# Reordered combinations, modulation rows first, score head pairs, and the state table loaded ahead of the lag table

## The reference, cut to what matters

```
# first block, 512 tokens x 1024 channels
proj = rms_norm(h) @ w_in                        # q, k, v, g, u
scores = einsum(q, k) * decay                    # 8 heads of 64
ret = silu(g) * group_norm(scores @ v)
h = h + concat([ret, pool_mixer(u)]) @ w_out
h = h + moe(rms_norm(h))                         # top 4 of 32 experts
gate = sigmoid(rms_norm(h, norm_ple_w) @ ple_gate_w)
h = h + gate * (p @ ple_proj_w)
x = rms_norm(h, final_norm_w)
# second block, layer 0: 64 groups of a complex state space model
u = modulate(rms_norm(x), shift, scale)
state_t = Abar * state_{t-1} + Bbar * u_t        # 64 states per group
y = gelu(Re(C state_t) + D * u_t)
x = x + g1 * (y @ w_out)[value * sigmoid(gate)]
# then feed-forward, short convolution, feed-forward, final norm
```

## Time and profile before

| | us |
|---|---|
| median of 3 runs | 2770.83 (2763.73 to 2775.92) |
| the profiled execution, its own time | 2767.87 |
| its span, first to last instruction | 2766.2 |
| PE busy in the span | 2596.2 |
| DVE busy | 1962.1 |
| ACT busy | 1352.4 |
| mean granted TensorE clock | 0.968 of full |

### The profile page before, as it was taken

How to read it: one execution, slowest core, us unless ns; L and a number is a source line. 1 busy time by engine, 2 the same in 40 slices (tenths; PEclk the granted TensorE clock), 3 DMA queues, 4 the chain that set the end, 5 groups by cost and what they waited for, 6 DMA issues and landing times.

```text
span 2766.2 us, 34756 instructions
## 1 busy us (share of the span) xinstructions
PE 2596.2 (94%) x12400; PEld 2103.0 (76%) x12400; DVE 1962.1 (71%) x1968; ACT 1352.4 (49%) x1346; POOL 187.7 (7%) x288
## 2 busy tenths in 40 slices
PE   5988889999999999999998786989999999999998
PEld 4767768888888888888886356878888787788886
DVE  5767789999999999999999877467743444533432
ACT  4232467777777777777776253322232222322322
POOL 1214010000000000000000200011100000000000
PEclk9999889999999999999999898999999999999999
DMA  6762599999999999999996932357743532133332
GB/s 231 259 209 48 208 343 389 381 382 381 384 379 380 380 383 383 384 381 380 382 379 231 181 86 71 81 152 227 222 108 87 145 91 76 31 100 97 97 105 73
DMA packets 364565, 642.30 MB, mean 232 GB/s; under 512 B 40908, under 2 KB 234132, under 8 KB 363732
## 3 DMA queue, kind: packets, MB, share of 16 engines
q1 hardware_dynamic: 341172, 541.28, 57.9%
q0 software_dynamic: 17296, 76.03, 8.0%
q10 hardware_dynamic: 6032, 24.12, 2.2%
HBM read 615.22 MB, written 26.68 MB: 232 GB/s over the span
## 4 chain that ended last, share of the span: by engine, by line
PE 85%; DVE 8%; DMA 3%; ACT 2%; issue 1%; POOL 0%; DVEq 0%; ACTq 0%; SPq 0%; POOLq 0%
PE bank L2384 38%; PE bank L2612 12%; PE bank L2613 12%; PE bank L2618 12%; PE bank L2484 1%; DMA cb<-in_w_ada 1%; PE bank L2359 1%; PE bank L2372 1%; PE bank L2366 1%; PE bank L2193 1%; PE bank L2244 1%; PE bank L2194 1%; PE bank L2195 1%; PE bank L2236 1%; DVE rows L1812 1%
## 5 line engine op out<-in xcount | busy, mean ns | idle before, releaser
L1709 DVE TENSOR_TENSOR slot_lo<-ring,slot_hi 128x2048 fp32r<-128x2048 f32 x384 | 864.0, 2284 | 84.0 <-ACT slot_hi L1001 82.8
L1001 ACT ACTIVATE slot_hi<-ring 128x2048 fp32r<-128x2048 f32 x384 | 736.3, 1920 | 283.9 <-PE bank L2384 259.2
L2384 PE MATMUL bank<-slot_hi,xs_hi 128*128 128x512 f32 x1024 | 324.5, 398 | 0.0
L2384 PE MATMUL bank<-slot_hi,xs_lo 128*128 128x512 f32 x1024 | 317.0, 391 | 0.0
L2612 PE MATMUL bank<-h_hi,fin_hi 128*128 128x512 f32 x704 | 277.3, 394 | 4.1 <-ACT h_hi L1214 3.4
L2613 PE MATMUL bank<-h_hi,fin_lo 128*128 128x512 f32 x704 | 275.6, 391 | 0.0
L2384 PE MATMUL bank<-slot_lo,xs_hi 128*128 128x512 f32 x1024 | 275.0, 390 | 0.0
L2384 PEld LDWEIGHTS bank<-slot_hi,xs_hi 128*128 128x128 f32 x1024 | 188.4, 189 | 51.7 <-issue 16.1
L2384 PEld LDWEIGHTS bank<-slot_hi,xs_lo 128*128 128x128 f32 x1024 | 193.4, 189 | 41.0
L2384 PEld LDWEIGHTS bank<-slot_lo,xs_hi 128*128 128x128 f32 x1024 | 192.7, 188 | 40.6 <-DVE slot_lo L1709 0.5
L1247 ACT ACTIVATE fin_hi<-rows 128x1024 fp32r<-128x1024 f32 x88 | 88.2, 1052 | 223.8 <-DMA rows<-in_w_ffn_in 223.8
(11 more groups left out here) (446 smaller groups left out, 4059.1 us busy)
## 6 DMA issues: line engine op xcount, KB each, us to landing
ring<-in_expert_w_gate_up SPq DMA_DIRECT2D x256, 1024.0 KB, 7.0
ring<-in_expert_w_down SPq DMA_DIRECT2D x128, 1024.0 KB, 6.6
rows<-in_w_ffn_in SPq DMA_DIRECT2D x88, 512.0 KB, 5.0
work<-in_w_ada POOLq DMA_DIRECT2D x64, 384.0 KB, 3.9
cb<-in_w_ada POOLq DMA_DIRECT2D x48, 384.0 KB, 4.5
y_dram<-cb ACTq DMA_DIRECT2D x32, 512.0 KB, 7.2
work<-in_w_ffn_out SPq DMA_DIRECT2D x8, 1408.0 KB, 7.0
rows<-in_w_ffn_out SPq DMA_DIRECT2D x8, 1408.0 KB, 6.9
```

The costliest lines, as they stand in the source:

```text
L1001: act.activation(hi_of(e, j), slot[q], ACT.Copy).then_inc(s_slot_hi, 1)
L1709: tt(slot_lo[:, q], slot[q], whole(hi_of(e, j)), ALU.subtract).then_inc(s_slot_lo, 1)
L2384: last = mm(ps[banks + n], x[:, k, :], (lo if lower else hi)[:, k, 512 * n:512 * (n + 1)], start=(begins and lower == 0 and k == 0 and x i ...
```

## The change

- **Scores in head pairs.** The two heads of a pair alternate, column block by column block, in banks 4/5 and 6/7. There are four score buffers instead of two, the last two in `nat`. Pair p+1 is issued in two halves, one ahead of each head's values. `mixed_low` calls are spread over the pairs.
- **Gate weights.** The first half of `ple_w_sb` is loaded once up step 5 of the last expert is done; the second half stays where it was.
- **Gathers.** `got[12..15]` are now the buffers `got[0..3]`, and the last four gathers wait for `combine(0)`. `ple_gate` on ACT loses its wait for all combinations, `out_square` gets it.
- **DVE order.** `c_power(4)` goes ahead of `combine(0)`; `ple_add(0)` ahead of `c_power(6)` and `(7)`.
- **SP order.** `mod_bc`, then both halves of the state table, then (after both have landed) the lag table. PE waits for it in `chunk_rows(0)`.

```diff
-        scr_s = [ring[:, 22016 + 1280 * b:22016 + 1280 * (b + 1)] for b in range(2)]
+        scr_s = [ring[:, 22016 + 1280 * b:22016 + 1280 * (b + 1)] for b in range(2)] + \
+                [nat[:, 1280 * b:1280 * (b + 1)] for b in range(2)]
...
-              [work[:, first:first + 1024] for first in (0, 1024, 6144, 7168)] + \
-              [nat[:, 1024 * n:1024 * (n + 1)] for n in range(4)]
+              [work[:, first:first + 1024] for first in (0, 1024, 6144, 7168)]
+        got += got[0:TOPK]
...
+            sp.wait_ge(s_slot_done, 12 * (E - 1) + 2)
+            load(ple_w_sb[0], ple_gate_v[:, :, 0:512], s_ple_in)
             load_down(E - 1, E - 1, 12 * (E - 1) + 5)
...
             load(p_rows, p_by_chunk, s_ple_in)
-            for n in range(2):
-                load(ple_w_sb[n], ple_gate_v[:, :, 512 * n:512 * (n + 1)], s_ple_in)
+            load(ple_w_sb[1], ple_gate_v[:, :, 512:1024], s_ple_in)
...
-            sp.wait_ge(s_k_out, 16 * (CH + 1))
-            sp.wait_ge(s_got_used, 3)
-            for v in range(CH):
-                load(m_t[GC * v:GC * (v + 1), :, :], kd[:, :, (CH - 1 - v) * GC:(2 * CH - 1 - v) * GC], s_t_in)
             sp.wait_ge(s_cols_ready, COLS_P)
             sp.wait_ge(s_got_used, NT)
             sp.wait_ge(s_side_in, 112)
...
                 load(mod_bc[v].rearrange("p g h -> p (g h)"), mod_dram[v].partition_broadcast(P), s_side_in)
             for half in range(2):
                 sp.wait_ge(s_pgate_ready, 2 * NT - 1 + half)
-                sp.wait_ge(s_t_in, 16 * (CH + half))
+                if half:
+                    sp.wait_ge(s_t_in, 16)
                 load(m_w[:, GP * half:GP * (half + 1), :],
                      m_w_dram.rearrange("p (g m) -> p g m", g=G)[:, GP * half:GP * (half + 1), :], s_t_in)
+            sp.wait_ge(s_t_in, 32)
+            sp.wait_ge(s_k_out, 16 * (CH + 1))
+            for v in range(CH):
+                load(m_t[GC * v:GC * (v + 1), :, :], kd[:, :, (CH - 1 - v) * GC:(2 * CH - 1 - v) * GC], s_t_in)
...
+                    if n == 3 * TOPK:
+                        pool.wait_ge(used, 1)
...
             def ple_gate(i, n):
...
-                if i:
-                    act.wait_ge(s_got_used, NT)
...
             def out_square(i):
                 act.wait_ge(s_pproj_taken, 2 * i + 2)
+                act.wait_ge(s_got_used, NT)
...
+            for pair in range(HEADS // 2):
                 for j in range(NT):
                     n = S - P * j
+                    for b in range(2):
+                        h = 2 * pair + b
+                        dve.wait_ge(s_score_ps, 2 * NT * pair + 2 * j + b + 1)
+                        if pair >= 2 and j == 0:
+                            dve.wait_ge(s_y_ps, h - 3)
+                        tt(scr_s[h % 4][:, SCORE_AT[j]:SCORE_AT[j] + n], ps[4 + 2 * (j % 2) + b][:, 0:n], decay[:, h, 0:n],
+                           ALU.mult).then_inc(s_score_sb, 1)
+
+                for n in ((0,), (1, 2), (), (3,))[pair]:
+                    mixed_low(n)
+                if pair == 2:
                     dve.wait_ge(s_sil, 1)
                     step(tt(silu_g, silu_g, proj[:, :, 3 * RET:4 * RET], ALU.mult))
...
+            c_power(4)
             combine_main(0)
             combine_main(1)
             ple_rstd(0, 1)
-            c_power(4)
             combine_main(2)
             ple_rstd(1, 2)
             c_power(5)
+            ple_add(0)
             c_power(6)
             c_power(7)
-            ple_add(0)
             combine_main(3)
...
+            def scores(pair, columns):
+                for j in columns:
+                    at = 2 * NT * pair + 2 * j - (4 if j >= 2 else 2 * NT - 4)
+                    if at >= 0:
+                        pe.wait_ge(s_score_sb, at + 2)
+                    for b in range(2):
+                        pp = slice(HD * b, HD * (b + 1))
+                        mm(ps[4 + 2 * (j % 2) + b][:, 0:S - P * j], cb3[pp, 4 + pair, P * j:P * (j + 1)], cb3[pp, pair, P * j:S],
+                           start=True, stop=True).then_inc(s_score_ps, 1)
...
-                pe.wait_ge(s_score_sb, NT * (h + 1))
+                pe.wait_ge(s_score_sb, 2 * NT * (h // 2 + 1))
...
+            scores(0, range(NT))
+            for pair in range(HEADS // 2):
+                for b in range(2):
+                    if pair + 1 < HEADS // 2:
+                        scores(pair + 1, (2 * b, 2 * b + 1))
+                    values(2 * pair + b)
...
             def chunk_rows(k):
                 pe.wait_ge(s_x_state, k // 2 + 1)
+                if k == 0:
+                    pe.wait_ge(s_t_in, 16 * (CH + 2))
```

More of the change, by code:

```diff
@@ L647, in _ @@
             with sp.If(extra > 0):
+                sp.wait_ge(s_ple_in, 16)
                 with sp.Fori(0, extra) as n:
@@ L651, in _ @@
                     load_down(n + E, expert, n * 12 + 12 * E - 3)
+                sp.wait_ge(s_slot_done, extra * 12 + 12 * E - 4)
+                load(ple_w_sb[0], ple_gate_v[:, :, 0:512], s_k_ps)
             sp.wait_ge(s_slot_done, extra * 12 + 12 * E - 4)
@@ L795, in _, with take @@
                     next_tile(n + E)
-            def take(source, index, done):
+            def take(source, index, done, used):
                 for n in range(NT * TOPK):
@@ L810, in _ @@
             with pool.If(extra > 0):
-                take(y_more, 36, [s_more_in] * NT)
+                take(y_more, 36, [s_more_in] * NT, s_more_used)
                 pool.wait_ge(s_more_used, NT)
-            take(y_dram, 20, s_got_in)
+            take(y_dram, 20, s_got_in, s_got_used)
             pool.wait_ge(s_hs_ready, KD)
@@ L1104, in _ @@
                     act.wait_ge(s_xst_ready, 2 * n + 2 * E + 4)
+                act.wait_ge(s_k_ps, 20)
             act.wait_ge(s_ple_in, 48)
@@ L1507, in _ @@
             dve.wait_ge(s_s5_in, 96)
-            for h in range(HEADS):
+            for pair in range(HEADS // 2):
                 for j in range(NT):
                     n = S - P * j
[L1511 to L1520, removed]
+                    for b in range(2):
[8 more added lines that the diff above has]
+                if pair == 2:
                     dve.wait_ge(s_sil, 1)
@@ L1879, in _ @@
                 main_step, step = step, Steps(dve, s_dve_more2)
-                dve.wait_ge(s_more_in, 16 * NT * TOPK)
                 for i in range(NT):
+                    if i == 0:
+                        dve.wait_ge(s_more_in, 16 * (NT - 1) * TOPK)
+                    if i == NT - 1:
+                        dve.wait_ge(s_more_in, 16 * NT * TOPK)
                     combine(i, more, s_more_used)
@@ L2243, in values @@
                         at = SCORE_AT[j] + P * (i - j)
-                        last = mm(ps[i][:, HD * h:HD * (h + 1)], scr_s[h % 2][:, at:at + P],
+                        last = mm(ps[i][:, HD * h:HD * (h + 1)], scr_s[h % 4][:, at:at + P],
                                   proj[:, j, 2 * RET + HD * h:2 * RET + HD * (h + 1)], start=(j == 0), stop=(j == i))
                 last.then_inc(s_y_ps, 1)
[L2248 to L2252, removed]
+            scores(0, range(NT))
[4 more added lines that the diff above has]
+                    values(2 * pair + b)
             def mixer_out(n, i, first, end):
@@ L2532, in chunk_sums @@
                 if b % 2 == 0:
-                    pe.wait_ge(s_t_in, 16 * (CH + 1 + b // 2))
+                    pe.wait_ge(s_t_in, 16 * (1 + b // 2))
                 for r in range(2):
```

## The result

The changed kernel takes 2775.44 us (median of 12 runs, 2770.2 to 2784.5), the kernel before 2770.51 (12 runs): ratio 1.002, 95% interval 1.0011 to 1.003, so 3 to 8 us slower. Its profiled execution has a span of 2773.3 us, 7.1 more than before.

A forecast was written before the change was run, and what follows sets the result against it. PE, with 85% of the chain, was taken to bound the kernel, mostly in untouched matmul streams. Scores -6.5 and the late lag table +7.5 (8.1 gained included) gave +1.0, 2768.9, or 2772 as median; range 2759 to 2784.

The forecast's parts named there:

- Scores, -6.5: Score stage: a pair's matmuls run side by side, 2.35 us instead of 4.70, ending the stage at 228.1, not 234.6.
- Rival B: Score stage: the head pairs don't overlap, +8.5 us in all, 2779; chance 0.12.
- Carries through to the experts unchanged: Score stage to experts: the full -6.5 us reaches the experts, since everything there is released relatively.
- Gate weights, -1.9: Last expert: early load takes 2 MB out of the way of the last `y_dram` store, 1.9 us gained, bounds 0 and 3.
- `c_power(4)`, -1.9: Combination: 3.8 us of DVE work move into the 5.63 us wait for gathered rows, gaining 1.9 us.
- `ple_add(0)` first: Combination and gates: PE's 6.27 us wait and slow product vanish; U columns come 8.1 us earlier, earlier edits included.
- Rival D: Gate stage: combination 3 or an ACT step replaces the removed wait, gates no faster; +11.5 us, 2782.3; chance 0.12.
- When the lag table goes out and lands: SP queue: eight loads go out after the state table, near 1607.6, need 46.0 us, land at 1660.1 less 6.5.
- Rival C: State stage: lag table arrives before 1641.5, hidden, needing 153 GB/s; -14.6 us, 2756.2; chance 0.12.
- chunk_rows(0) is ready at 1641.5 and waits 18.6 us, PE idle: State stage: PE waits for the late lag table, so recurrence 2 starts at 1674.5 instead of 1667.0, +7.5 us.
- the missing gap: State stage sign: a PE gap of about 19 us before `chunk_rows(0)`, ended by DMA; its absence would mean Rival C.
- A: Whole kernel, main forecast: +1.0 us, own range 2767 to 2782; chance 0.60.

The follow-up runs named there:

- experiment 6: Changed kernel, eight lag loads replaced by same bytes in 512-byte pieces over all 128 partitions, read from the state table in DRAM (wrong data): ratio 0.9968.
- experiment 3: Kernel before with only SP's new queue order and the moved waits: ratio 1.0076, 21 us slower.
- experiment 4: Changed kernel without the eight lag loads and without PE's wait for them: ratio 0.9958.
- experiment 5: Changed kernel with four of the eight lag loads left out, half the table keeping old data: ratio 0.9979.
- experiment 8: Changed kernel with the eight lag loads behind `mod_bc`, ahead of the state table, wait counts set back: ratio 0.9984.
- experiment 9: Changed kernel with lag loads early, right behind the modulation rows, and cut into 32 interleaved loads: 2758.18 us, ratio 0.9961.
- experiment 7: Changed kernel with each lag load cut into four, 32 loads in turn over eight blocks of 16 partitions: ratio 1.0003.

## Why the prediction was right, step by step

The range (2759 to 2784) held the time, 2775.44, and the change is small as forecast, but +3 to +8 us where +1.0 was forecast, and one mechanism was not what I described.

- **Scores, -6.5: right in the stage.** First values 202.92 (forecast 202.8), evictions 227.71 (228.1), -6.7 with the start taken into account. Rival B, no overlap, is refuted. "Carries through to the experts unchanged" was wrong by about 1 us: DVE's group norm meets POOL's powers. In whole times the edit alone gave 2 and 4 us.
- **Gate weights, -1.9: right**, 2.1. **`c_power(4)`, -1.9: too much**, 1.1, since the gathers came earlier than I allowed and the wait that it hides in had shrunk to 1.3 us.
- **`ple_add(0)` first: right.** PE's wait and slow product are gone. From the last down loads to the U columns it is 142.0 before and 133.3 after, -8.7 (forecast -8.1) for the three edits together; with 2.1 and 1.1 for the other two some 5.5 are left for this one, which no run takes alone. Rival D, in which the gates don't get faster, is refuted.
- **When the lag table goes out and lands: right.** Issued at 1607.82 (forecast 1607.6); DMA falls silent at 1654.1 (1660.1 - 6.5 = 1653.6). Rival C, hidden at 153 GB/s, is refuted for loads like these. The Trainium skill (DMA: Bandwidth & Descriptors, Specifications) gives 512 bytes as the smallest transfer at line rate. Pieces of that size moved at 289 GB/s in experiment 6, with 128 partitions per load, and at 94 here with 16, so a piece of 512 bytes is not enough for a high rate.
- **The failed step: "chunk_rows(0) is ready at 1641.5 and waits 18.6 us, PE idle".** It assumed that PE runs its chunk sums beside the loads as fast as alone. It doesn't: three stops of 19.0 us together (8.09 + 7.98 + 2.92) come in front, and behind each of them matmuls run at half clock (granted 0.50 from 1628.7 to 1631.2 and from 1642.9 to 1648.6, 0.51 from 1656.3 to 1659.0). From the first U column to `chunk_rows(0)` it is 22.2 us before and 47.0 after; 19.0 of the 24.8 are stops, the other 5.8 slower matmuls. At 1659.0, when PE gets to `chunk_rows(0)`, the table has lain there for 5 us.

  I had named the missing gap as the sign of C; here it was a sign of neither A nor C. That the sizes agree (18.6 and 19.0) is half chance: by the code PE would have waited for the table anyway, so whatever ends before it lands costs nothing extra, and only the 5 us beyond 1654 were new. After that two chunk rows and what follows took 12.7 us instead of my 14.4: I had taken the rows from behind a wait, where they start at half clock (8.2 us), and here PE came straight from work and ran them at full clock (1659.03 to 1665.73, 6.7 us). So 5.4 - 1.7 = 3.7 us, just the difference between recurrence 2 at 1671.72 and my 1674.5 - 6.5 = 1668.0. With the forecast's 1.0 and the 2.4 of "the rest" that makes the 7.1 us between the two profiles.

What is shown: the stops exist only where lag loads run beside the chunk sums (experiments 3, 4, 5, 8, 9), always at the same point of a block, and shrink when the loads are spread (6, 7). With each stop beside narrow loads goes an instruction packet that begins 8 to 9 us late (4 to 8 in experiment 7), and PE goes on 3 to 4 us after it. What is argued: that this packet, or the request for it, waits behind the lag table's writes. The Trainium skill (DMA: Bandwidth & Descriptors, Back-pressure in remote DMA) says that a saturated destination port clogs the path back, and that stalled writes stall an engine's other queues too; it says so of transfers between cores. The late packets here would fit it for loads from DRAM, but no view shows a port or what the request waits for. What fills the 3.8 us between the packet (1624.9) and PE's next matmul (1628.71) no view shows either.

## What to carry to other kernels

A transfer that moves from beside long matmuls to beside hundreds of short ones can stop the engine through its instruction fetch; look for "issue" gaps in the middle of a block, and for the instruction queue's packet in that window. Before moving a load, look at how many partitions it writes: over 16 of them it ran at 94 GB/s here, and what is hurt by it is not only its own reader. Where a load must be narrow, issue it early and cut it into pieces that alternate over the partitions.

## What the runs showed of the hardware that I had not expected

- 16 KB instruction packets, one per 64 U-column and 64 chunk-sum matmuls. PE, which runs such a block in 5 us, has a reserve of less than one block. In experiment 6 (289 GB/s on 128 partitions) a packet 1.7 us later than usual cost nothing and one 2.9 us late cost 1.06 us; in the changed kernel (94 GB/s on 16) one 8.8 us late cost 8.1.
- The rate of 512-byte pieces: 94 to 97 GB/s over 16 partitions, 119 with 32 loads interleaved over eight blocks of 16, 289 over 128 (from another DRAM tensor).
- DVE's 128x2048 products took 2.83 us instead of 2.29 beside POOL's, and POOL's 128x256 products 2.67 instead of 0.74.
- PE's mean granted clock from the first U column to `ssm_w_out` was 0.78 in the changed kernel, 0.87 before and 0.87 without lag loads. Behind the stops of 8.09 and 7.98 us PE ran at the lower of the two levels, granted 0.50: 2.61 us for 44 chunk sums, where 44 at full clock, behind a stop of 3.03 us in experiment 7, took 1.50.
